# Row transfers in place of single floats, and feed forward's first buffers loaded in the mixers' last iteration

## What is computed

```
h = rmsnorm(x, g_mix) * (1 + sc1) + sh1
proj = h @ w_in                                   # 1024 x 3340, split among the mixers
y_a = band attention over 512 past tokens and the own chunk, learned bias
y_b = mLSTM with matrix state c, vector state n, running maximum m
y_c = causal conv of width 4 on x/B/C, then SSD with state h (ssm)
y_d = gated by a lower triangular 128 x 128 matrix
x = x + gt1 * (concat(y_a, y_b, y_c, y_d) @ w_out)
h2 = rmsnorm(x, g_ffn) * (1 + sc2) + sh2
g, u = h2 @ f_w_gate, h2 @ f_w_up                 # 1024 x 2816 each
x = x + gt2 * ((silu(causal_dwconv3(g)) * u) @ f_w_down)
y = rmsnorm(x, g_final)
```

## Time and profile before

| | us |
|---|---|
| median of three runs | 3125.38 |
| lowest and highest | 3123.64, 3128.56 |
| the profiled execution | 3130.59 |
| its span, first to last instruction | 3128.8 |
| PE busy | 2858.1 (91%) |
| DVE busy | 1297.4 (41%) |
| ACT busy | 982.2 (31%) |
| mean granted clock of PE | 0.953 |

### The profile page before, as it was taken

How to read it: one execution, slowest core, us unless ns; L and a number is a source line. 1 busy time by engine, 2 the same in 40 slices (tenths; PEclk the granted TensorE clock), 3 DMA queues, 4 the chain that set the end, 5 groups by cost and what they waited for, 6 DMA issues and landing times.

```text
span 3128.8 us, 41943 instructions
## 1 busy us (share of the span) xinstructions
PE 2858.1 (91%) x16292; PEld 2559.3 (82%) x16292; DVE 1297.4 (41%) x2483; ACT 982.2 (31%) x1682; POOL 245.2 (8%) x413
## 2 busy tenths in 40 slices
PE   4599999999567999996799999999999989999987
PEld 1288888999455788885799998799999879999975
DVE  1333334432244554543333345444433544544444
ACT  0133334332221444443222224332222433222333
POOL 0000000000023332321000000000000000000000
PEclk8699999999777999998899999999999999999998
DMA  9622225212566443431522225433222443322344
GB/s 290 221 79 95 93 82 160 88 67 71 100 147 211 134 142 120 134 110 57 144 61 61 67 61 168 149 107 94 60 67 60 154 148 113 110 74 74 101 142 129
DMA packets 342122, 355.35 MB, mean 114 GB/s; under 512 B 44407, under 2 KB 283515, under 8 KB 341540
## 3 DMA queue, kind: packets, MB, share of 16 engines
q1 hardware_dynamic: 332642, 351.26, 36.6%
q10 hardware_dynamic: 9348, 2.29, 0.4%
HBM read 285.62 MB, written 70.10 MB: 114 GB/s over the span
## 4 chain that ended last, share of the span: by engine, by line
PE 48%; DMA 2%; DVE 1%; SPq 1%; issue 1%; ACT 0%; POOL 0%; DVEq 0%
PE acc_ps L2858 14%; PE acc_ps L2816 11%; PE acc_ps L2814 11%; PE acc_ps L2815 11%; DMA w_raw<-in_f_w_down 1%; DMA xr<-scratch_x 0%; DVE y L3106 0%; SPq L2758 0%; DMA out_y_prompt<-y 0%; DVE xr L3100 0%; DMA ffn_gate_in<-scratch_ffn_gate 0%; DVE prod L3094 0%; DVE w_lo L3023 0%; DVE w_lo L3080 0%; DVE mid L3124 0%
## 5 line engine op out<-in xcount | busy, mean ns | idle before, releaser
L2814 PE MATMUL acc_ps<-h_hi,w_hi 128*128 128x384 f32 (+1 forms) x2112 | 689.7, 327 | 6.2 <-DVE w_lo L3023 6.2
L2815 PE MATMUL acc_ps<-h_lo,w_hi 128*128 128x384 f32 (+1 forms) x2112 | 689.2, 326 | 0.0
L2816 PE MATMUL acc_ps<-h_hi,w_lo 128*128 128x384 f32 (+1 forms) x2112 | 689.1, 326 | 0.0
L3023 DVE TENSOR_TENSOR w_lo<-w_raw,w_hi 128x1024 fp32r<-128x1024 f32 x242 | 296.4, 1225 | 664.3 <-ACT w_hi L2911 654.6
L2911 ACT ACTIVATE w_hi<-w_raw 128x1024 fp32r<-128x1024 f32 x242 | 256.5, 1060 | 801.4 <-PE acc_ps L2816 522.6
L2814 PEld LDWEIGHTS acc_ps<-h_hi,w_hi 128*128 128x128 f32 x2112 | 397.6, 188 | 7.4 <-DVE w_lo L3023 6.6
L2815 PEld LDWEIGHTS acc_ps<-h_lo,w_hi 128*128 128x128 f32 x2112 | 397.4, 188 | 0.1
L2816 PEld LDWEIGHTS acc_ps<-h_hi,w_lo 128*128 128x128 f32 x2112 | 397.4, 188 | 0.0
L2858 PE MATMUL acc_ps<-w_hi,mid_hi 128*128 128x512 f32 x748 | 238.1, 400 | 31.1 <-DVE mid_lo L3073 15.7
L2858 PE MATMUL acc_ps<-w_lo,mid_hi 128*128 128x512 f32 x748 | 235.2, 396 | 0.0
L2858 PE MATMUL acc_ps<-w_hi,mid_lo 128*128 128x512 f32 x748 | 234.3, 395 | 0.0
(11 more groups left out here) (488 smaller groups left out, 4174.1 us busy)
## 6 DMA issues: line engine op xcount, KB each, us to landing
w_raw<-in_f_w_down SPq DMA_DIRECT2D x122, 512.0 KB, 3.6
w_raw<-in_f_w_gate SPq DMA_DIRECT2D x66, 512.0 KB
w_raw<-in_f_w_up SPq DMA_DIRECT2D x66, 512.0 KB, 3.9
w_ada<-in_w_ada SPq DMA_DIRECT2D x12, 2048.0 KB
m_bc<-scratch_bc SPq DMA_DIRECT2D x16, 768.0 KB, 5.1
scratch_tok<-p_m SPq DMA_DIRECT2D x17, 640.0 KB, 3.0
m_tok<-scratch_tok SPq DMA_DIRECT2D x16, 640.0 KB, 4.7
scratch_ht<-p_m SPq DMA_DIRECT2D x17, 512.0 KB, 3.9
```

Source lines behind the costliest of these rows:

```text
L2814: t.matmul(dst, hi, h2_hi[:, k, cols], start=(k == 0), stop=False)
L2815: t.matmul(dst, hi, h2_lo[:, k, cols], start=False, stop=False)
L2816: last = t.matmul(dst, lo, h2_hi[:, k, cols], start=False, stop=(k == KD - 1))
L3023: v.tensor_tensor(w_lo[j][:], raw[j][:], w_hi[j][:], ALU.subtract).then_inc(s_lo[j], 1)
```

## The change

Single floats become rows. The last conv rows are transposed by PE, copied by DVE and stored as one transfer. The samples' n comes in as rows of 64 floats (n_rows, twice side by side), is transposed by PE ahead of scores(0) and copied into cst by DVE behind m_done; turn_ssm and old_c wait for that. On the way out PE transposes it behind the last attention, DVE copies it to n_out ahead of add_h, and one transfer stores it. The taps come as rows of 128 and are transposed with the history.

Transfers are joined or moved: the bias goes in two, V in four; s_b_c is stored before the last pair of ya, and ssm by head, as each head is added. The mixers' first bc, band and the first gate are issued by ACT.

Feed forward's buffers (feed_forward_tiles) are allocated over the storage of the programs before it, in an order in which the first loads fall on buffers that the mixers no longer use in iteration 16. SP issues these loads (FirstLoads) there, and behind them the prompt's states. The mixers' program no longer awaits its stores; SP does so in feed forward at its third slice, and DVE after the sixth. The transposed prompt state is made within iteration 16 and kept in wt.

```diff
-            sp.wait_ge(s_cv, KX * NGR)
-            for n in range(3):
-                sp.dma_start(O["p_c_conv"][0, 0, n].rearrange("(k p) -> p k", p=P), xbuf[:, :, TW + n],
-                             allow_slow_non_contiguous=True).then_inc(s_copy, 16)
+            sp.wait_ge(s_ctk, 4)
+            sp.dma_start(O["p_c_conv"][0, 0], last_rows).then_inc(s_copy, 16)
...
                     v.tensor_copy(conv_rows[:, 512:768], f_ps[0:3 * NB, 0:256]).then_inc(s_ctk, 1)
+            dve.wait_ge(s_ct, 3)
+            v.tensor_copy(last_rows[:, 0:512], aux[0:3, :])
+            v.tensor_copy(last_rows[:, 512:768], f_ps[0:3, 0:256]).then_inc(s_ctk, 1)
...
+            for k in range(KX):
+                to = aux[0:3, k * P:(k + 1) * P] if k < 4 else f_ps[0:3, (k - 4) * P:(k - 3) * P]
+                last = t.transpose(to, xbuf[:, k, TW:TW + 3], c["ident"][:])
+            last.then_inc(s_ct, 1)
...
+            def load_v(j):
+                sp.dma_start(v_in[:, 2 * j:2 * j + 2], A["cache_a_v"][0, 2 * j:2 * j + 2].rearrange(
+                    "b (p n) h d -> p b n (h d)", p=P)).then_inc(s_v[j], 16)
...
+            for b2 in range(2):
+                sp.dma_start(bias_in[b2 * DH:(b2 + 1) * DH, :], rel_tile(S, slice(0, TS), slice(0, SB)).rearrange("t h j -> h t j")
+                             ).then_inc(E["bias_loaded"], 16)
+            for r in range(2):
+                sp.dma_start(n_rows[:, r * DH:(r + 1) * DH], A["state_b_n"][0].rearrange("b h d -> (b h) d")
+                             ).then_inc(E["n_in"], 16)
...
                              ).then_inc(E["cst_loaded"], 16)
-                sp.dma_start(cst[half(h), h // 2, :, DH], A["state_b_n"][0, :, h].rearrange("b d -> d b"),
-                             allow_slow_non_contiguous=True).then_inc(E["cst_loaded"], 16)
...
+            for j in range(NG - 1):
+                store_ya(j)
             sp.wait_ge(E["c_added"], 4)
             for h in range(H):
-                sp.dma_start(O["s_b_n"][0, :, h].rearrange("b d -> d b"), cst[half(h), h // 2, :, DH],
-                             allow_slow_non_contiguous=True).then_inc(E["stored"], 16)
...
                              ).then_inc(E["stored"], 16)
-            sp.wait_ge(E["h_added"], H)
-            for b in range(NB):
-                sp.dma_start(O["s_c_ssm"][0, b].rearrange("h p n -> p h n"), ssm[half(b), b // 2]).then_inc(E["stored"], 16)
-            sp.wait_ge(E["stored"], 16 * (2 + NB + 2 * H + NB))
+            store_ya(NG - 1)
+            sp.wait_ge(E["n_out"], 1)
+            sp.dma_start(O["s_b_n"][0].rearrange("b h d -> b (h d)"), n_out[:]).then_inc(E["stored"], 16)
+            for h in range(H):
+                sp.wait_ge(E["h_added"], h + 1)
+                for r in range(2):
+                    sp.dma_start(O["s_c_ssm"][0].rearrange("(g r) h p n -> r h p g n", r=2)[r, h], ssm[half(r), :, h, :]
+                                 ).then_inc(E["stored"], 16)
+            sp.wait_ge(E["stored"], 16 * (2 + NB + 1 + H + 2 * H))
...
+                pe.wait_ge(E["n_kept"], 2)
...
+                pe.wait_ge(E["cst_loaded"], 16 * H)
+                pe.wait_ge(E["n_kept"], 2)
                 pe.wait_ge(E["ssm_kept"], NG)
...
+            pe.wait_ge(E["n_in"], 32)
+            t.transpose(m[:, B_B, 0:NB * H], n_rows[:], ident[0:NB * H, 0:NB * H]).then_inc(E["n_turned"], 1)
...
+            pe.wait_ge(E["c_added"], 4)
+            for a in range(2):
+                last = t.transpose(m[0:NB, B_Q, a * P:(a + 1) * P], cst[:, a, :, DH], ident[:])
+            last.then_inc(E["n_back"], 1)
...
+            dve.wait_ge(E["n_turned"], 1)
+            for r in range(2):
+                v.tensor_copy(cst[half(r), :, :, DH], m[half(r), B_B, 0:NB * H].rearrange("p (b a r) -> p r a b", b=NB, r=2)[:, r]
+                              ).then_inc(E["n_kept"], 1)
+            dve.wait_ge(E["bias_loaded"], 16 * 2)
...
+            dve.wait_ge(E["n_back"], 1)
+            v.tensor_copy(n_out[:], m[0:NB, B_Q, 0:GW]).then_inc(E["n_out"], 1)
...
+            def load_feed_forward():
+                sp.wait_ge(E["h2_stored"], 16 * (NT - 1))
+                sp.wait_ge(E["max_done"], H * NT)
...
+                sp.wait_ge(E["y_turned"], 2 * NM)
+                ffn_first.load(sp)
+
+            def store_states():
...
+                sp.wait_ge(E["ssm_kept"], 1)
+                sp.dma_start(O["p_c_ssm"][0, 0].rearrange("h p n -> p h n"), wt[0:DH]).then_inc(E["finals"], 16)
...
-            load_bc(0)
             sp.dma_start(k_t[:, :, 0:512], S["ka"][:, :, 0:512]).then_inc(s_k[0], 16)
-            sp.dma_start(band[:], rel_tile(S, slice(0, P), slice(0, BAND))).then_inc(E["band_loaded"], 16)
...
-            sp.dma_start(gate[:], S["mix_gate"][:, 1, :]).then_inc(E["gate_loaded"], 16)
...
+                if n == NT:
+                    load_feed_forward()
+                    store_states()
...
-            sp.wait_ge(E["finals"], 16 * (2 * H + 1))
-            sp.wait_ge(s_x2[0], 16 * (NM // 2 + 1))
-            sp.wait_ge(s_x2[1], 16 * (NM // 2))
-            sp.wait_ge(E["h2_stored"], 16 * NM)
+
+        def stored(engine):
...
+                if o == NT:
+                    turn_states()
...
+            transfer_bc(act, 0)
+            act.dma_start(band[:], rel_tile(S, slice(0, P), slice(0, BAND))).then_inc(E["band_loaded"], 16)
+            act.dma_start(gate[:], S["mix_gate"][:, 1, :]).then_inc(E["gate_loaded"], 16)
...
+                if o == NT:
+                    dve.wait_ge(E["ssm_turned"], 1)
+                    v.tensor_copy(wt[0:DH], m[0:DH, 0, :].rearrange("p (h n) -> p h n", h=H)).then_inc(E["ssm_kept"], 1)
...
+    def load(self, sp):
+        A, F = self.A, self.F
+        for n in range(4):
+            sp.dma_start(F["h2_first"][:, 2 * n:2 * n + 2, :], self.S["h2t"][:, 2 * n:2 * n + 2, 0:MAXT]).then_inc(self.h2[n], 16)
+            if n == 0:
+                for j, name in enumerate(("f_w_gate", "f_w_up")):
+                    sp.dma_start(F["raw"][j][:].rearrange("p (k c) -> p k c", k=KD),
+                                 A[name][0].rearrange("(k p) (f c) -> f p k c", p=P, c=P)[0]).then_inc(self.raw[j], 16)
+                sp.dma_start(F["rows_in"], A["state_ffn_conv"][0].rearrange("b j n -> (b j) n")).then_inc(self.hist, 16)
+                for j in range(3):
+                    sp.dma_start(F["tap_rows"][j * KF:(j + 1) * KF], A["f_conv_w"][0, j].rearrange("(f p) -> f p", p=P)
+                                 ).then_inc(self.taps, 16)
+                sp.dma_start(F["tap_rows"][3 * KF:4 * KF], A["f_conv_b"][0].rearrange("(f p) -> f p", p=P)).then_inc(self.taps, 16)
...
-            def load_gu(s, f, first=False):
+            def load_gu(s, f):
                 for j, w in enumerate((wg, wu)):
-                    if not first:
-                        sp.wait_ge(s_lo[j], unit(s, f))
...
-            for n in range(4):
-                sp.dma_start(h2_first[:, 2 * n:2 * n + 2, :], S["h2t"][:, 2 * n:2 * n + 2, 0:MAXT]).then_inc(s_h2f[n], 16)
...
-                    sp.dma_start(rows_in, A["state_ffn_conv"][0].rearrange("b j n -> (b j) n")).then_inc(s_hist, 16)
-            for j in range(3):
-                sp.dma_start(taps[:, :, j], A["f_conv_w"][0, j].rearrange("(f p) -> p f", p=P),
-                             allow_slow_non_contiguous=True).then_inc(s_par, 16)
-            sp.dma_start(taps[:, :, 3], A["f_conv_b"][0].rearrange("(f p) -> p f", p=P),
...
                     if s or f:
                         load_gu(s, f)
+                    if s == 0 and f == 2:
+                        m_stored(sp)
+                        sp.dma_start(g_fin[:], A["g_final"].partition_broadcast(P)).then_inc(s_par, 16)
+                        sp.dma_start(ffn_gate[:], S["ffn_gate"]).then_inc(s_par, 16)
...
             pe.wait_ge(s_hist, 16)
+            pe.wait_ge(s_taps, 16 * 4)
             for f in range(KF):
-                last = t.transpose(acc[:, 3, 0, f * 16:(f + 1) * 16], rows_in[:, f * P:(f + 1) * P], c["ident"][0:16, 0:16])
-            last.then_inc(s_ht, 1)
...
+            v.tensor_copy(hist[:], acc[:, 3, 0, 0:KF * 16].rearrange("p (f n) -> p f n", f=KF))
+            v.tensor_copy(taps[:], acc[:, 3, 0, KF * 16:KF * 20].rearrange("p (j f) -> p f j", j=4)).then_inc(s_hk, 1)
...
-            dve.wait_ge(s_par, 16 * 6)
+            dve.wait_ge(s_hk, 1)
...
+                if s == 0:
+                    m_stored(dve)
+                    dve.wait_ge(s_par, 16 * 2)
```

## The result

| | us |
|---|---|
| the changed kernel: median of four runs (lowest, highest) | 3075.51 (3071.06, 3083.00) |
| the kernel before, all its runs by then: median of four | 3124.51 (3117.65, 3128.56) |
| ratio, 95% interval | 0.9837 (0.9816 to 0.9858) |
| the profiled execution, and its span | 3078.29, 3076.6 |
| mean granted clock of PE | 0.963 |

The account below looks back on a forecast made before the run. PE bounds most of the kernel, but the DMA queue and SP's issues and waits bound two stretches, sample stage and seam. -17.5 - 10 - 1 - 26.3 = -54.8 gives 3075.8 profiled, 3070.6 us as median; range 3059 to 3087.

Parts of the forecast that it names:

- A: Sample stage up to old_c: first loads no longer queue behind single-float stores; -17.5 us, bounds -13 and -20.
- Every landing 15.5 us earlier: Sample stage's first loads: with the queue free, each landing moves from after 836.4 to after 821 us.
- s_cst landing: Sample stage: s_cst lands at 845, or 842.2 us once state_b_n's floats, some 2.8 us, drop out of the loads.
- n_kept path at "843": Sample stage: turn_ssm's new wait for DVE's n_kept, then ACT's keeping, brings this path to old_c at 843 us.
- B: End of the sample stage: DVE's w_out_lo, not SP's stores, is last; -10 us, bounds -11 and -5.
- Rival 2: Sample stage's end: s_b_c's 256 B runs stay dear, so B is only -5, time 3075.6 us; chance 0.1.
- C: Mixers' start: first bc, band and gate issued on ACT's queue instead of SP's; -1 us, bounds -2.6 and +3.
- nothing to gain: Mixers' start: first scores need band, through after about 4.4 MB instead of 4.0 MB, so no gain there.
- D: Seam from mixers to feed forward: early loads, moved wait, taps as rows; -26.3 us, bounds -20 and -28.
- rival 3: Mixers' iteration 16: the queue fills, store_h2(16) slips 8 us, D is -18, time 3079 us; chance 0.08.
- The clock: Whole kernel: PE, granted 0.50 to 0.58 in three windows, will idle less; range includes 5 us this may bring.
- Rival 4: Feed forward: buffers at other addresses make its 8580 matmuls dearer, +86 us at +10 ns each, 3156 us; chance 0.03.

Follow-up runs that it names:

- e6: The changed kernel with V of streams 0 and 1 loaded behind the samples' matrix state instead of ahead of it; 3068.59 us, ratio 0.9819.
- e1: The kernel before with only the last conv rows (p_c_conv) turned by PE and stored as three rows; 3110.06 us against 3127.48, ratio 0.9938.
- e2: The changed kernel with s_b_n stored again as four columns of single floats, each ahead of its s_b_c; 3078.58 us, ratio 0.9845.
- e4: The kernel before with only feed forward's taps and bias loaded as rows and turned by PE; 3123.10 us against 3127.48, ratio 0.9989.
- e5: The changed kernel with SP awaiting the mixers' last stores again at the end of the mixers' program; 3085.34 us, ratio 0.9860.
- e8: The changed kernel with feed forward's first loads issued behind the mixers' loop, after the last h2 store; 3088.62 us, ratio 0.9872.
- e3: The changed kernel with the mixers' first bc, band and gate issued by SP at their old places; 3078.72 us, ratio 0.9837.
- e7: The changed kernel with w_out's low part made in the mixers' program, behind the columns of bc; 3084.18 us, ratio 0.9857.
- e10: The changed kernel with w_out's low part made as DVE's first work in the mixers' program, ahead of the columns of bc; 3072.18 us, ratio 0.9835.
- e11: The changed kernel again, unaltered, measured as reference on the same chip as two variants; 3076.76 us, ratio 0.9842.

## Why the prediction was right, and where its steps were off

**What bounds.** Right. Of the signs named, mix_in comes 7.2 us after s_tok (7 forecast), old_c 27.6 (24 forecast, as in e6), the first matmul 8.23 after the last h2 store (8 forecast), and w_out_lo ends the stage. The queue held the first loads and the stage's last stores (e1, e2), and the seam was made of issues, a wait and late loads (e4, e5, e8).

**A** was mis-sized: 13.4 (14.1 by the clock of the trace), not 17.5. "Every landing 15.5 us earlier" held at mix_in (825.91 against 825.6) but not further down: s_cst was there at 846.36, not at 842.2. The step that failed is the s_cst landing, and most of it the 2.8 us for state_b_n's floats: I took their price from the taps' issue time, and e1, which still loads them, shows that they cost nothing where they stood. The other 1.4 us stay open. From mix_in to old_c the kernel before takes 19.4 us, e4 (the same code there) 21.0, e1 18.9, and the eight profiles with the changed kernel's order of loads (after, e2, e3, e5, e7, e8, e10, e11) 20.0 to 22.1: the list with fewer issues and no floats was not faster, and the 1.4 us lie within that spread. The n_kept path at "843" was right to 0.4 us, as e6 shows, where V no longer stands ahead of s_cst; in the kernel before V stood there as well. The bound of -13 covered it.

**B** was right, -10.6 for -10, and by the mechanism named: DVE's w_out_lo ends the stage. n_out's copy cost nothing: from DVE's first add_h to w_out_lo it is 3.9 us with it and without it, for the adds wait for PE. Rival 2 (short runs of s_b_c) falls: s_b_c is stored in the same runs and SP is done before DVE. The Trainium skill (DMA: Bandwidth & Descriptors, Specifications) puts line rate at 512 B and above; here the loads in runs of 512 B go at 175 GB/s (up to 238 from 848 to 850 us of the kernel before) and those of 4 KB at 423, with the engines as busy, so the trace doesn't bear that bound out.

**C** had the wrong sign: I gave -1, the trace +1.2, and e3 gets 1.5 back. The step that failed is "nothing to gain" for the band bytes set against a gain at bc: the bytes from ACT's queue delay xc and k_t, which PE needs first, and bc wasn't what the first product waited for. The Trainium skill (DMA: Bandwidth & Descriptors, Rules for kernel authors) says that a second queue brings no bandwidth and that the queues' transfers interleave on the same engines. e3 agrees, and adds the price of it: 19.4 us to the first product with one queue, 21.0 with two.

**D** was right to 1.1 us. That 1.1 is rival 3 in small: I set SP's 14.9 us of issues against an interval of 15.3 and left out store_x(16). The issues took 15.8 us (to 1443.46) and store_x(16) another 0.6, so the h2 store was issued 1.2 us after its data. "It costs nothing" for the moved wait was right, but I had taken the old wait of 7 us for its worth; behind the early loads it would have been 9.9 (e5).

**The clock** I had put in the range as a possible gain. It went both ways: +2.8 between old_c and w_out_lo, where PE was at 0.50 from 896 to 904 us, and -6.4 in the mixers, of which 4.7 are the stretch shown under e11. Between profiles of the same code both come and go: old_c to w_out_lo is 65.6 us in e11 too, at a mean clock of 0.73 there, but 63.2 in e8, which has the same code there, at 0.78. Without the two stretches the terms add up to -48.6; the medians say -49.0 (first runs) and -47.3 (beside e11). So it is partly luck that the two profiles, 52.3 us apart, come so near the sum of 54.8: the terms by themselves were some 6 us too hopeful, 4.1 of it in A and 2.2 in C.

**Rival 4** (other addresses) falls: feed forward from its second group on takes 1613.35 us against 1613.25.

## To carry to other kernels

A few thousand single floats stored late in one program are paid for by the first loads of the next: look for full DMA engines that move few bytes, then make rows of the floats with a transpose on an idle engine. When loads are pulled ahead of a barrier, take the wait for the last stores out of it as well, or the stores, now behind the loads, give part of the gain back (9.9 us here). In a queue that never runs dry, what PE needs first must be issued first; a second queue, or a big transfer one place too early, delays it.

## What the runs showed of the hardware

- Single floats are dear on the way out. 2304 of them held the first loads back by 14.6 us (e1: 7.0 us from s_tok's issue to the first work, where it was 21.6), some 6.4 ns each. Packets of the kernel before in three windows (816 to 820, 820 to 824, 828 to 832 us):

```profile
DMA packets 2496, 0.21 MB, mean 52 GB/s; under 512 B 2368, under 2 KB 2496, under 8 KB 2496
DMA packets 0, 0.00 MB, mean 0 GB/s; under 512 B 0, under 2 KB 0, under 8 KB 0
DMA packets 36, 0.18 MB, mean 46 GB/s; under 512 B 0, under 2 KB 0, under 8 KB 36
```

  The floats' own packets are over by 820 us; then no packet is recorded for 4 us, and after that the loads crawl until the floats have landed (by 836.4). In the third window, with a DMA share of 1.16 of 16 engines, a packet takes 2.1 us; at 852 to 856 us of the changed kernel it takes 0.15 us (450 packets, share 1.03). So the price does not show in the floats' packets but in the loads behind them; what the engines wait for there no row shows. On the way in 2535 small packets took 3 us (e1).
- Two queues, one set of engines: five transfers on ACT's queue delayed SP's first transfer by 2.3 us and its k_t by 4.5 (e3).
- DVE's subtraction of two SBUF tiles took 1.15 us alone (9.17 for eight, e10) and 1.76 us on the mean beside POOL (14.07, e7). The Trainium skill (SBUF — State Buffer, Who interferes with whom) says that a DVE instruction with two SBUF inputs contends with a GpSimd instruction that reads SBUF. e7 and e10 agree: POOL's small operations, too, take 1.6 us each in e7 and 0.6 in e10, where DVE's subtractions are over by then.
- PE's granted clock is at 0.50 (1.2 GHz) from 1000 to 1008 us of the kernel before and from 980 to 988 us of e11, with PE busy all the time, and at 1.00 at the same place in the changed kernel's first profile. At 1.00 it is 2.4 GHz. Just ahead of that place PE had waited for DVE in all three, 1.65 us (before, to 999.11), 1.73 (e11, to 978.52) and 1.92 (to 978.11) in the profile without the stretch. What decides it stays open; it was not tried.
